# The two 16-column projections turned round: the activations stationary, the weights moving

## The reference, cut to what matters

```python
# first block, GLA mixer: the last 16 columns of w_in
proj = h @ w_in
q, k, v, r, g_low = jnp.split(proj, [...], axis=-1)           # g_low: 256 x 16
log_a = jax.nn.log_sigmoid((g_low @ w_gate_up + b_gate)) / GLA_GATE_TEMP

# second block, hybrid mixer: 8 columns a and 8 columns b of w_in
# (sizes 3072, 1024, 8, 8, 512, ...): the decay and beta of the gated delta rule
```

## Time and profile before

| | |
|---|---|
| median of 3 runs | 2499.22 us (2499.2 to 2499.51) |
| the profiled execution's own time | 2499.43 us |
| its span, first to last instruction | 2497.6 us |
| TensorE busy with matmuls | 2485.2 us, 12518 matmuls |
| VectorE, ScalarE busy | 1486.3 us, 1520.8 us |
| mean granted clock of TensorE | 0.999 |
| DMA | 472 MB, mean 189 GB/s |

### The profile page before, as it was taken

The page is one execution under the profiler, slowest core; times in us unless marked ns, Lnnn a source line. Parts: engine busy times, 40 slices in busy tenths (PEclk is TensorE's granted clock), DMA queues, the critical chain, the costliest instruction groups (busy, mean ns, idle before and its releaser), DMA issues.

```text
span 2497.6 us, 29737 instructions
## 1 busy us (share of the span) xinstructions
PE 2485.2 (100%) x12518; PEld 2053.8 (82%) x12518; DVE 1486.3 (60%) x1220; ACT 1520.8 (61%) x1993; POOL 33.4 (1%) x41
## 2 busy tenths in 40 slices
PE   9999999999999999999999999999999999999998
PEld 7787788888888888888888888888888888888887
DVE  5855656544545545666765665545565667646674
ACT  6545677636637547776465565545586688538863
POOL 0000000000000000000000000000000000000000
PEclk9999999999999999999999999999999999999999
DMA  8554455555555555545444445555655555555554
GB/s 286 185 187 168 174 205 200 187 200 186 201 186 200 188 199 188 197 174 186 153 161 145 153 164 189 197 191 195 260 192 180 186 194 194 187 200 186 200 187 152
DMA packets 69366, 472.37 MB, mean 189 GB/s; under 512 B 7912, under 2 KB 8352, under 8 KB 13424
## 3 DMA queue, kind: packets, MB, share of 16 engines
q1 hardware_dynamic: 67040, 460.62, 51.6%
q0 software_dynamic: 1312, 7.73, 0.8%
q10 hardware_dynamic: 880, 2.11, 0.2%
HBM read 468.33 MB, written 2.11 MB: 188 GB/s over the span
## 4 chain that ended last, share of the span: by engine, by line
PE 97%; DVE 1%; ACT 1%; issue 1%; DMA 0%; SPq 0%; POOLq 0%; POOL 0%; DVEq 0%; ACTq 0%
PE acc L530 31%; PE acc L531 31%; PE acc L532 31%; PE tp L550 1%; PE tp L820 1%; DVE w_lo L1695 0%; PE tp L753 0%; DMA x_raw<-in_x_turned 0%; DVE kT L1855 0%; PE tp L692 0%; PE tp L701 0%; DVE cv L1984 0%; ACT w_hi L1053 0%; PE tp L565 0%; PE tp L566 0%
## 5 line engine op out<-in xcount | busy, mean ns | idle before, releaser
L1695 DVE TENSOR_TENSOR w_lo<-w_raw,w_hi 128x2048 fp32r<-128x2048 f32 x430 | 983.4, 2289 | 728.5 <-ACT w_hi L1053 726.6
L1053 ACT ACTIVATE w_hi<-w_raw 128x2048 fp32r<-128x2048 f32 x430 | 822.9, 1915 | 498.9 <-DMA w_raw<-in_stream 468.3
L530 PE MATMUL acc<-w_hi,x_hi 128*128 128x512 f32 (+1 forms) x2240 | 875.1, 391 | 2.4 <-DVE w_lo L1695 2.0
L531 PE MATMUL acc<-w_lo,x_hi 128*128 128x512 f32 (+1 forms) x2240 | 868.4, 388 | 0.0
L532 PE MATMUL acc<-w_hi,x_lo 128*128 128x512 f32 (+1 forms) x2240 | 868.4, 388 | 0.0
L530 PEld LDWEIGHTS acc<-w_hi,x_hi 128*128 128x128 f32 x2240 | 420.6, 188 | 91.8 <-DVE w_lo L1695 2.8
L532 PEld LDWEIGHTS acc<-w_hi,x_lo 128*128 128x128 f32 x2240 | 420.6, 188 | 86.4
L531 PEld LDWEIGHTS acc<-w_lo,x_hi 128*128 128x128 f32 x2240 | 420.7, 188 | 85.3 <-issue 1.0
L530 PE MATMUL acc<-w_hi,a_hi 128*128 128x512 f32 x1120 | 436.8, 390 | 0.1
L531 PE MATMUL acc<-w_lo,a_hi 128*128 128x512 f32 x1120 | 435.8, 389 | 0.0
L532 PE MATMUL acc<-w_hi,a_lo 128*128 128x512 f32 x1120 | 435.8, 389 | 0.0
(11 more groups left out here) (388 smaller groups left out, 1289.7 us busy)
## 6 DMA issues: line engine op xcount, KB each, us to landing
w_raw<-in_stream SPq DMA_DIRECT2D x430, 1024.0 KB, 4.8
w_raw<-in_stream SPq DMA_DIRECT2D x16, 256.0 KB, 7.6
h<-in_x SPq DMA_DIRECT2D x4, 512.0 KB, 13.5
frow<-in_rows POOLq DMA_DIRECT2D x2, 1024.0 KB, 7.3
m_raw<-in_mem_turned POOLq DMA_DIRECT2D x1, 2048.0 KB, 9.5
memt<-in_mem POOLq DMA_DIRECT2D x1, 2048.0 KB, 10.1
x_raw<-in_x_turned SPq DMA_DIRECT2D x3, 512.0 KB, 7.8
dec<-gc_rows ACTq DMA_DIRECT2D x1, 1024.0 KB, 6.3
```

Of the source, the lines that this page charges most:

```text
L530: pe.matmul(dst, xh, wh[:, k], start=first and k == 0, stop=False)
L531: pe.matmul(dst, xh, wl[:, k], start=False, stop=False)
L1053: act.activation(w_hi[:, c % SLOTS], w_raw[:, c % SLOTS], ACT.Copy).then_inc(hi_ready, 1)
L1695: dve.tensor_tensor(w_lo[:, c % SLOTS], w_raw[:, c % SLOTS], w_hi[:, c % SLOTS].bitcast(F32), ALU.subtract).then_inc(lo_ready, 1)
```

## The change

x becomes the stationary operand (128 x 128) and the 32 or 16 weight columns move. For each half m of the tokens there are 16 times two matmuls, 64 for a projection where there were 32, and they write rows of tokens straight away. `sixteen_rows_back` and its two groups are gone. In their place the high and low halves of the result are added by VectorE: ScalarE copies both halves to SBUF (`glow_parts` at c == 3; `ab_parts` at c == 4, with the rows scaled) and one VectorE addition each makes `glow16` (at its c == 6) and `ab` (at its c == 4). ScalarE waits for the first through `glow_sum`, TensorE waits for the scaled rows through `glow_ready`. As two groups fall out of the plan, the later ones change their places in the alternation.

```diff
--- before.py
+++ after.py
@@ -109,7 +109,8 @@
         wg_raw = sb("wg_raw", [P, 16, 16], F32, a_s + 32 * K)
         wg = sb("wg", [P, 16, 32], F32R, a_s + 33 * K)
         glow = sb("glow", [P, M, 4, 32], F32, a_s + 35 * K)
-        glow_rows = sb("glow_rows", [32, SEQ], F32, a_s + 42 * K)
+        glow_parts = sb("glow_parts", [P, M, 32], F32, a_s + 42 * K)
+        glow16 = sb("glow16", [P, M, 16], F32, a_s + 42 * K + 256)
         glowT = sb("glowT", [P, SEQ], F32, a_s + 36 * K)
         w_gu = sb("w_gu", [P, 1024], F32, a_s + 37 * K)
         zb = sb("zb", [P, 8, SEQ], F32, a_a)
@@ -165,7 +166,7 @@
         gc_rows = nc.dram_tensor("gc_rows", (8, SEQ), F32, kind="Internal").ap()
         wab_raw = sb("wab_raw", [P, 16, 16], F32, a_s + 45 * K)
         wab2 = sb("wab2", [P, 16, 32], F32R, a_s + 46 * K)
-        ab_rows = sb("ab_rows", [32, SEQ], F32, a_s + 40 * K)
+        ab_parts = sb("ab_parts", [P, M, 32], F32, a_s + 40 * K)
         cv = sb("cv", [P, 4, SEQ], F32, a_a + 8 * K)
         th = sb("th", [P, 4, SEQ], F32, a_a + 12 * K)
         zz = sb("zz", [P, M, 1024], F32, a_a + 8 * K)
@@ -224,7 +225,7 @@
         hi_ready, lo_ready, used = sem("hi_ready"), sem("lo_ready"), sem("used")
         tp_done = sem("tp_done")
         took = {k: {e: [sem(f"{k}_took_{e}{p}") for p in range(2)] for e in ("act", "dve")} for k in ("acc", "tp")}
-        cols_in, cst_in, mask_in, gla_in, row_in, out_done = [sem(s) for s in ("cols_in", "cst_in", "mask_in", "gla_in", "row_in", "out_done")]
+        cols_in, cst_in, mask_in, gla_in, row_in, out_done, glow_sum, glow_ready = [sem(s) for s in ("cols_in", "cst_in", "mask_in", "gla_in", "row_in", "out_done", "glow_sum", "glow_ready")]
         x_in = sem("x_in")
         w_part = [[sem(f"w_part{c}_{k}") for k in range(4)] for c in range(EARLY)]
         gain_in, xT_in, x0_high, x0_low = sem("gain_in"), [sem(f"xT_in{n}") for n in range(NB + 1)], sem("x0_high"), sem("x0_low")
@@ -309,7 +310,7 @@
             for n in range(4):
                 add_quarter(j, n)
 
-        for name, who in (("glow_rows", "act"), ("glow", "act"), ("glowT", "act"), ("z0", "act"), ("z1", "act")):
+        for name, who in (("glow", "act"), ("glowT", "act"), ("z0", "act"), ("z1", "act")):
             tps.add(name, who)
         for hd in range(4):
             tps.add(("s", hd), "act")
@@ -356,7 +357,7 @@
 
 
         add_quarter(3, 3)
-        add("ab_rows", "ab", who="act")
+        add("ab", who="act")
         add(("dT", 0))
         add(("nN", 0), who="act")
         add("gc")
@@ -561,26 +562,16 @@
 
                 g = tps.name[name]
                 open_group(g)
-                for k in range(16):
-                    pe.matmul(tp[0:32, g % 2, 0, :], w[:, k], x_hi[:, k, :], start=k == 0, stop=False)
-                    mm = pe.matmul(tp[0:16, g % 2, 0, :], w[:, k, 0:16], x_lo[:, k, :], start=False, stop=k == 15)
-                mm.then_inc(tp_done, 1)
-
-            def sixteen_rows_back(name, src_name, src):
-
-                g = tps.name[name]
-                open_group(g)
-                tps.wait(pe, tps.name[src_name])
                 for m in range(M):
-                    for half in range(2):
-                        mm = pe.matmul(tpf(g)[:, 16 * m:16 * m + 16], src[:, m * P:(m + 1) * P], ident[0:32, 16 * half:16 * half + 16],
-                                       start=half == 0, stop=half == 1)
+                    dst, own = tpf(g)[:, m * N:m * N + 32], slice(m * P, (m + 1) * P)
+                    for k in range(16):
+                        pe.matmul(dst, x_hi[:, k, own], w[:, k], start=k == 0, stop=False)
+                        mm = pe.matmul(dst[:, 0:16], x_lo[:, k, own], w[:, k, 0:16], start=False, stop=k == 15)
                 mm.then_inc(tp_done, 1)
 
             def low_rank_transposed():
                 g = tps.name["glowT"]
                 open_group(g)
-                tps.wait(pe, tps.name["glow"])
                 for m in range(M):
                     mm = pe.transpose(tp[:, g % 2, 0, m * P:(m + 1) * P], glow[:, m].rearrange("p r n -> p (r n)"), ident)
                 mm.then_inc(tp_done, 1)
@@ -649,11 +640,10 @@
                 chunk(C_GLA + c, X, 4 * q, accs.name[("gla", b)], q == 0, q == 3)
                 if c == 3:
                     pe.wait_ge(wg_l, 1)
-                    sixteen_columns("glow_rows", wg)
-                if c == 6:
+                    sixteen_columns("glow", wg)
+                if c == 8:
                     pe.wait_ge(cst_in, 16)
-                    sixteen_rows_back("glow", "glow_rows", glow_rows)
-                if c == 8:
+                    pe.wait_ge(glow_ready, 1)
                     low_rank_transposed()
                 if c == 10:
                     gate_logits()
@@ -707,9 +697,7 @@
             def dn_side(c):
                 if c == 3:
                     pe.wait_ge(wg_l, 2)
-                    sixteen_columns("ab_rows", wab2)
-                if c == 4:
-                    sixteen_rows_back("ab", "ab_rows", ab_rows)
+                    sixteen_columns("ab", wab2)
                 if c == 24:
                     pe.wait_ge(conv_out, 5)
                     back(("vN", 4), lambda hh: cv[:, hh])
@@ -1196,17 +1184,16 @@
                         act.wait_ge(scale_ready, SCALES[0])
                     row_scaled(0, dst, acc[:, n % 2]).then_inc(accs.sem(n), 1)
                     if n == 0:
-                        g = tps.name["glow"]
-                        act.wait_ge(tp_done, g + 1)
+                        act.wait_ge(glow_sum, 1)
                         act.wait_ge(pool_set, 2)
                         for m in range(M):
-                            ins = act.activation(glow[:, m, :, 0:16], tpf(g)[:, 16 * m:16 * m + 16].unsqueeze(1).to_broadcast([P, 4, 16]), ACT.Copy,
+                            ins = act.activation(glow[:, m, :, 0:16], glow16[:, m].unsqueeze(1).to_broadcast([P, 4, 16]), ACT.Copy,
                                                  scale=rstd[:, 0, m:m + 1])
-                        ins.then_inc(tps.sem(g), 1)
+                        ins.then_inc(glow_ready, 1)
                 if c == 3:
-                    g = tps.name["glow_rows"]
+                    g = tps.name["glow"]
                     act.wait_ge(tp_done, g + 1)
-                    act.activation(glow_rows[:], tp[0:32, g % 2, 0, :], ACT.Copy).then_inc(tps.sem(g), 1)
+                    act.activation(glow_parts[:], tpf(g).rearrange("p (m n) -> p m n", m=M)[:, :, 0:32], ACT.Copy).then_inc(tps.sem(g), 1)
                 if c == 8:
                     g = tps.name["glowT"]
                     act.wait_ge(tp_done, g + 1)
@@ -1321,7 +1308,7 @@
                 if c == 4:
                     g = tps.name["ab"]
                     act.wait_ge(tp_done, g + 1)
-                    row_scaled(3, ab, tpf(g)[:, 0:32].rearrange("p (m n) -> p m n", m=M)).then_inc(tps.sem(g), 1)
+                    row_scaled(3, ab_parts, tpf(g).rearrange("p (m n) -> p m n", m=M)[:, :, 0:32]).then_inc(tps.sem(g), 1)
                 def strips(name, dst):
                     for half in range(2):
                         g = tps.name[(*name, half)]
@@ -1384,9 +1371,6 @@
                                 hd = 4 * (b - 2) + hh
                                 act.activation(kdec[:, 0, hd * P:(hd + 1) * P], tpf(g)[:, hh * P:(hh + 1) * P], ACT.Copy, scale=ekd[:, 0, hd:hd + 1])
                         act.activation(flat(th[:]), tpf(g), ACT.Square).then_inc(tps.sem(g), 1)
-                if c == 3:
-                    g = tps.name["ab_rows"]
-                    take(g, ab_rows[:], tp[0:32, g % 2, 0, :])
                 if c == 4:
                     act.wait_ge(smalls_in, 48)
                     act.wait_ge(u_ready, 1)
@@ -1858,6 +1842,8 @@
 
             for c in range(64):
                 if c == 6:
+                    tps.wait(dve, tps.name["glow"])
+                    dve.tensor_tensor(glow16[:], glow_parts[:, :, 0:16], glow_parts[:, :, 16:32], ALU.add).then_inc(glow_sum, 1)
                     row_scales(0, 0)
                 if c in (8, 10, 12, 24):
                     n = (8, 10, 12, 24).index(c)
@@ -1962,6 +1948,7 @@
                     row_scales(3, 3)
                 if c == 4:
                     tps.wait(dve, tps.name["ab"])
+                    link(dve.tensor_tensor(ab[:], ab_parts[:, :, 0:16], ab_parts[:, :, 16:32], ALU.add))
                     dve.wait_ge(smalls_in, 48)
                     dve.tensor_tensor(u8[:], ab[:, :, 0:8], dtb.unsqueeze(1).to_broadcast([P, M, 8]), ALU.add).then_inc(u_ready, 1)
                 if c == 5:
```

## The result

| | before | after |
|---|---|---|
| median | 2499.57 us (6 runs, 2499.2 to 2499.95) | 2515.84 us (6 runs, 2514.33 to 2516.2) |
| ratio | | 1.0064, 95% interval 1.0054 to 1.0074 |
| profiled execution, span | 2499.43 us, 2497.6 us | 2516.20 us, 2514.4 us |
| mean granted clock of TensorE | 0.999 | 0.995 |

The change costs 16.3 us, 0.65%, clear of noise. The forecast was +4.6 us with a range up to 2507; the measured time lies outside it, and almost on the figure of the first rival, 2516 us. (In the new file the wide matmuls stand at L531 to L533, the narrow ones at L568 and L569.)

The account below looks back on a forecast made before the run. TensorE was taken to bound the kernel: two projections at +3.46 us each, less 2.35 us for the turnings back, made +4.6 us, forecast 2503.8 us on the median's scale, range 2501.0 to 2507.0.

Parts of the forecast that it names:

- the first rival: TensorE's clock falls during the narrow matmuls of each projection: +12.2 us on top of +4.6, 2516 us; chance 0.12.
- What goes: Both turnings back leave TensorE, 1.21 + 1.14 = 2.35 us; the old narrow products go too, 2 × 3.66 us.
- What comes, at full clock: 64 load-bound narrow matmuls per projection on TensorE, pitch 0.110 to 0.112 us: 7.12 us against 3.66, +3.46 each.
- The upper end of 0.120: Pitch of matmuls with 128 stationary and 256 moving columns: 7.76 us per projection, sum +5.9 us.
- the term of 7.12 us: Price of one projection's 64 new matmuls on TensorE, taken from the row for loads alone, with the last open load.
- The falling clock: Array slows toward 1.2 GHz in mid-group: other half 3.5 us longer, chunk behind loses 2.6 us, per projection; chance 0.12.
- What lies beside: Shifted ScalarE copy and scaling, VectorE additions, transfers and the stall near 101 us cost nothing; cover left before chunk 6's split 1.3 us.
- rival 3: TensorE's waits for w_lo, 2.8 us in all, take up part of the cost: +1.8 us left, 2501 us; chance 0.06.
- rival 2: The new loads on TensorE come at 0.062 us, 4.05 us a group: sum −1.6 us, 2498 us; chance 0.06.
- rival 4: Each new matmul on TensorE becomes two, 128 loads more: +14 us, 2518 us; chance 0.02.

Follow-up runs that it names:

- dve_back: Kernel before with its narrow products kept, but the turning back moved from TensorE to VectorE, with the scaling of `ab`; 2497.35 us, ratio 0.9991.
- spread8: Kernel after with its narrow matmuls cut into pieces of 8, one behind each block of six wide matmuls; 2505.34 us, ratio 1.0025.
- spread16: Kernel after with its narrow matmuls cut into pieces of 16, one behind every second block of six wide matmuls; 2505.51 us, ratio 1.0023.
- wide256: Kernel after with the moving weights repeated eight times, 256 and 128 columns instead of 32 and 16, same loads; 2505.09 us, ratio 1.0023.
- wide128: Kernel after with the moving weights repeated four times, 128 and 64 columns instead of 32 and 16, same loads; 2512.07 us, ratio 1.0054.
- halves: Kernel after with each narrow group in two halves of 32 matmuls, behind chunk 3 and behind chunk 4; 2510.59 us, ratio 1.0048.
- first_only: Kernel after with only the first projection in the new form, the second as in the kernel before with its turning back; 2508.54 us, ratio 1.0034.

## Why the prediction was wrong

**What goes** was right: 2.35 us by the rows, 2.2 us by dve_back.

**What comes, at full clock,** was right: a pitch of 0.110 to 0.112 us was forecast, and the narrow matmuls of the kernel after have (32.67 − 30.29)/22 = 0.108 with the first one, 0.112 from the second on. The upper end of 0.120 was not reached. spread8 and spread16, where the clock holds, show the forecast's mechanism nearly alone: +6.1 and +5.9 us, against +4.6. The pieces account for +4.9 of it in the trace of spread8; the rest is not assigned.

**Which case it was** is the step that failed: both groups were priced at the full clock. In the sum it is the term of 7.12 us for a projection. The two groups took 11.2 us (41.52 − 30.29) and 10.4 us (1121.72 − 1111.37), with the granted clock at 0.50 from 32.8 and 1114.9 us on, and the chunks behind them lost another 2.4 and 1.7 us. The falling clock had its chance of 0.12 from this sentence: "Against it: projection and chunks stand without a gap, and the loads are dense." Both halves are true of the trace and neither counted. The clock fell with PE and PEld busy for the whole stretch, and wide256, with the same loads, kept it. The prediction had said in the same paragraph that the trace has nothing like seven microseconds of narrow matmuls; the longest run was 1.29 us. It also leaned on the row of the granted clock, which it found nowhere under full. But that row reads 1.00 in the kernel before from 2 to 7 us too, where 16 matmuls take 0.40 us each, so it can miss a slow stretch; in the stretches around the projections clock and pitch agree. A case for which the trace has no row near it can't be held to 0.12 by an argument on busy time. The range left it out altogether.

**The price of that rival** was nearly right, +12.2 on top of +4.6. Its parts are other than thought. I let the clock fall in mid-group; it fell after about 23 of 64 matmuls in the first group and 31 in the second, which costs 41 × 0.101 = 4.1 and 33 × 0.101 = 3.3 us, against 3.5 each. The wide matmuls behind lost 5.12 − 12 × 0.227 = 2.4 and 3.47 − 8 × 0.227 = 1.7 us, against 2.6 each. Together 11.5.

**What lies beside** held, though one cover did go, a case that the prediction had thought through. ScalarE's copy waited 8.3 us for the slow group, and the split of chunk 6 came 2.8 us later than the 39.06 of the earlier trace rows:

```profile
41.71 0.22 ACT L1196 ACTIVATE glow_parts<-tp 128x64 f32<-128x64 f32 x1 [8.29 <-PE tp L569]
41.83 3.70 ACT L1041 ACTIVATE w_hi<-w_raw 128x2048 fp32r<-128x2048 f32 x2
```

TensorE did not wait for it. Its waits after the start are those of before: the longest, for w_lo near 100 us, is still 1.7 us. So rival 3 (the stall swallows part) did not occur; nor did rival 2 (cheap loads; they last 0.19 us at full clock) or rival 4 (the 48 more matmuls are 64 more narrow ones, less the 16 rows of the turning back).

**What stays open.** wide128, wide256 and the runs in pieces bracket the case on two sides, in the columns that move and in the length of the run. They don't say what the chip measures, and the time from the start of a narrow run to the fall differed from 2.5 to 4.8 us between groups and executions.

## What to carry to other kernels

In this kernel a matmul goes by its longer side: with a load of 128 columns the pitch is about 0.11 us for up to 128 moving columns, and 0.227 us for 512. Then ask separately what the array streams: here a run of 64 or 32 full loads with 16 or 32 moving columns each lost the clock although PE showed busy throughout, and the wide work behind the run paid too. Keep the small operand stationary and the long one moving; if narrow matmuls can't be avoided, cut the run and put it between wide ones (runs of 8 and 16 kept the clock here), and read the granted clock in stretches of 2 us, not on the page's forty slices.

## What the runs showed that was not expected

- Adding work of no use made the kernel faster. Above the kernel before on the same chip, it costs 16.3 us with 32 and 16 moving columns per load, 12.8 us with 128 and 64, and 5.9 us with 256 and 128.
- At the lower clock the loads slow down as well: those of the first group last 0.333 us in the slow part against 0.19 before it, and the narrow pitch goes from 0.112 to 0.213. A group bound by loads is thus no shelter from the clock. By source line, with shortest, median and longest duration in ns:

```profile
L568 PEld LDWEIGHTS tp<-wg,x_hi x32: 187/333/339, 30.1 to 41.0; 128*128 128x128 f32 x32
```

- The clock took 4.8 us of wide matmuls to come back after the first group and 3.1 after the second, counted from the first wide matmul to the first short pitch. In the traces of wide128, halves and first_only it took between some 2.5 and 5.7 us.
